# Tokens on two queues, a diagonal in place of scaled tokens, and other numbers of clock products in a two-block forward pass

## The reference

```
# first block
h = concat(meta, x)
xn = rms_norm(h, norm_mix);  proj = xn @ w_in
q, k, v, rw, gate_sb, gate_rw = split(proj)
y_sb = stick_breaking_attention(q, k, v)          # 8 heads
r, kr, vr, w_lo, a_lo, g_lo = split(token_shift(rw))
g = sigmoid(g_lo) @ g_up
y_rw = (group_norm(rwkv7_recurrence(...)) + bonus) * g
h = h + (sigmoid(gate_sb) * (y_sb @ w_sb_out) + sigmoid(gate_rw) * (y_rw @ w_rw_out)) @ w_out
h = h + swiglu(rms_norm(h) @ w_ffn_in) @ w_ffn_out
x = rms_norm(h, norm_final)[16:]
# second block
h = layer_norm(x, ln_in)                           # n = 0
for l in range(2):
    qkv = h @ w_in_2[l];  o = two kinds of attention, normed by head
    h = layer_norm(4 ** 0.25 * h + o @ w_o_2[l], ln1[l])       # n = 1, 3
    w = gelu(h @ u[l]) * gates of the chosen experts
    h = layer_norm(4 ** 0.25 * h + w @ v[l], ln2[l])           # n = 2, 4
return h
```

## Time and profile before

| | |
|---|---|
| device time, median of 3 runs | 2400.44 us (2398.69 to 2403.57) |
| the profiled execution | 2400.53 us |
| its span, from the first to the last instruction | 2398.7 us |
| busy: PE, PE weight loads, DVE, ACT, POOL | 98%, 87%, 70%, 54%, 24% |
| mean granted TensorE clock | 0.996 |
| DMA | 420.99 MB, 176 GB/s in the mean |

### The profile page before, as it was taken

The page is one execution under the profiler, slowest core; times in us unless marked ns, Lnnn a source line. Parts: engine busy times, 40 slices in busy tenths (PEclk is TensorE's granted clock), DMA queues, the critical chain, the costliest instruction groups (busy, mean ns, idle before and its releaser), DMA issues.

```text
span 2398.7 us, 42228 instructions
## 1 busy us (share of the span) xinstructions
PE 2347.3 (98%) x16485; PEld 2095.4 (87%) x16485; DVE 1684.5 (70%) x3068; ACT 1301.3 (54%) x2800; POOL 573.9 (24%) x440
## 2 busy tenths in 40 slices
PE   8999999999999999999999999999999999999998
PEld 7878989997899889999888887789989999888886
DVE  5745354446689778887776556869888888777556
ACT  6543345456564665545555555655665555555554
POOL 3626135555379000000000003378300000000000
PEclk9999999999999999999999999999999999999999
DMA  5311155554245556556776564245555656777554
GB/s 200 116 62 47 54 167 188 187 185 147 75 159 178 190 182 197 193 198 206 244 245 215 193 213 151 82 159 172 182 191 192 194 193 197 237 245 236 194 193 159
DMA packets 148150, 420.99 MB, mean 176 GB/s; under 512 B 15984, under 2 KB 49136, under 8 KB 147568
## 3 DMA queue, kind: packets, MB, share of 16 engines
q1 hardware_dynamic: 144080, 405.34, 51.9%
q0 software_dynamic: 2256, 8.99, 1.0%
q10 hardware_dynamic: 1616, 3.96, 0.4%
HBM read 400.40 MB, written 17.83 MB: 174 GB/s over the span
## 4 chain that ended last, share of the span: by engine, by line
PE 93%; DVE 3%; ACT 2%; POOL 1%; DMA 1%; issue 1%; ACTq 0%; DVEq 0%; SPq 0%
PE pb L465 92%; PE pb L474 1%; POOL lo L2635 1%; ACT arena L1334 1%; ACT hi L1322 0%; DVE arena L2284 0%; ACT arena L1528 0%; DMA cst<-in_consts 0%; DMA raw<-in_w_out 0%; DVE arena L1880 0%; DMA raw<-in_w_ffn_in 0%; DVE arena L1877 0%; DVE arena L2345 0%; ACT HT L1334 0%; ACT L1334 0%
## 5 line engine op out<-in xcount | busy, mean ns | idle before, releaser
L465 PE MATMUL pb<-HT,hi 128*128 128x256 f32 (+2 forms) x5232 | 1093.8, 302 | 3.9 <-POOL lo L2635 1.9
L1322 ACT CAST hi<-raw 128x512 fp32r<-128x512 f32 x1402 | 821.0, 620 | 372.8 <-PE pb L465 255.7
L465 PEld LDWEIGHTS pb<-HT,hi 128*128 128x128 f32 x5232 | 839.0, 191 | 42.6 <-issue 4.3
L465 PE MATMUL pb<-HT,lo 128*128 128x256 f32 (+1 forms) x2968 | 839.3, 283 | 0.0
L2635 POOL TENSOR_TENSOR lo<-raw,hi 128x512 fp32r<-128x512 f32 x384 | 525.3, 1390 | 437.1 <-ACT hi L1322 436.8
L1887 DVE TENSOR_TENSOR lo<-raw,hi 128x1024 fp32r<-128x1024 f32 x464 | 567.4, 1223 | 41.6 <-ACT hi L1322 41.4
L465 PEld LDWEIGHTS pb<-HT,lo 128*128 128x128 f32 x2968 | 566.6, 191 | 0.0
L465 PE MATMUL pb<-hi,WH 128*128 128x512 f32 x1112 | 433.2, 390 | 1.6 <-DVE WL L2569 1.1
L465 PE MATMUL pb<-lo,WH 128*128 128x512 f32 x1112 | 432.9, 389 | 0.0
L465 PE MATMUL pb<-hi,WL 128*128 128x512 f32 x1112 | 432.6, 389 | 0.0
L1334 ACT ACTIVATE arena<-pb 128x256 f32<-128x256 f32 (+2 forms) x216 | 82.4, 382 | 358.6 <-PE pb L465 355.6
(11 more groups left out here) (213 smaller groups left out, 2107.9 us busy)
## 6 DMA issues: line engine op xcount, KB each, us to landing
raw<-in_uT SPq DMA_DIRECT2D x256, 512.0 KB, 3.5
raw<-in_vT SPq DMA_DIRECT2D x256, 512.0 KB, 3.7
raw<-in_w_ffn_in SPq DMA_DIRECT2D x44, 512.0 KB, 3.8
raw<-in_wq SPq DMA_DIRECT2D x32, 512.0 KB, 3.5
wk<-kept SPq DMA_DIRECT2D x128, 128.0 KB, 3.5
raw<-in_w_in SPq DMA_DIRECT2D x24, 512.0 KB, 3.6
raw<-in_w_ffn_out SPq DMA_DIRECT2D x22, 512.0 KB, 4.4
raw<-in_w_gate SPq DMA_DIRECT2D x16, 512.0 KB, 3.2
```

What stands on the lines that cost most here:

```text
L465: return e.matmul(o, l, r, start=start, stop=stop)
L1322: e.copy(u.hi[k], u.half[k]).then_inc(*s.up("hi", ("hi", g)))
```

## The change

- **Start.** Block 0, meta tokens, identity and pack are loaded by ACT in this order; block 1 goes to SP's queue, in front of the weights. POOL waits for block 1 before it issues its four loads. ACT squares only block 0; the mean squares of the meta tokens and of block 1 come from DVE's bn statistics (mean squared plus variance). The tokens are no longer scaled into `xs`: DVE scales the identity into three diagonals `DG`, and PE multiplies the raw tokens (stationary) with the diagonal (moving), which turns and scales in one fp32 product. 18 clock products for 16.
- **Clock products.** Two before each of the four gate sums and two behind `att_c(0)` to `att_c(2)` are new; 44 for 100 at n=0, 20 for 40 at n=1 and n=3, 24 for 50 at n=2.
- **Low parts.** Of the second `w_in` unit of each layer both halves go to POOL.
- **Norms n=1, 3.** Block 0 is closed and scaled before the statistics of piece (1,1); ACT takes two roots; DVE scales (1,0), and ACT only (1,1).
- **Norm n=4.** Gain and bias go into the normalisation: per piece DVE does (x - mean) * gain and then * 1/root + bias, and no other engine works on it.

```diff
-                    low=both if (i, g) < (0, 2) else pool)
+                    low=both if (i, g) < (0, 1) else pool)
...
     w.wait_ge(*s.to("ident"))
-    warm(7, 16)
+    warm(7, 18)
     for c in range(8):
         b = c % 4
         emptied(b)
-        w.wait_ge(*s.to("xs"))
+        w.wait_ge(*s.to("diag"))
         for i, (o, n) in enumerate(BLK):
-            x = tp(PB[b][:, o:o + n], m.xs[0:n, i, c * 128:(c + 1) * 128])
+            x = mm(PB[b][:, o:o + n], m.tok[i][0][:, c * 128:(c + 1) * 128], m.DG[0:n, i * 128:i * 128 + n], True, True)
...
     for f in range(4):
         b, cs = SIDE + f, slice(f * 128, (f + 1) * 128)
         emptied(b)
+        for _ in range(2):
+            mm(PB[b][:, 256:512], m.one[:, 0:128], m.one, True, True)
         w.wait_ge(*s.to("g2"))
...
     for h in range(8):
         att_c(h)
-        if h > 2:
+        if h < 3:
+            warm(2, 2)
+        else:
             att_y(h - 3)
...
-    warm(2, 50)
-    warm(3, 50)
+    warm(2, 22)
+    warm(3, 22)
...
-        warm(2, 20)
-        warm(3, 20)
+        warm(2, 10)
+        warm(3, 10)
...
-            warm(2, 25)
-            warm(3, 25)
+            warm(2, 12)
+            warm(3, 12)
...
     e.dma_start(m.Hv[:, 0, :], rows[:, 0, :]).then_inc(*s.up("x0_in", ("x", 0), by=16))
-    e.dma_start(m.Hv[:, 1, :], rows[:, 1, :]).then_inc(*s.up("x1_in", ("x", 1), by=16))
     e.dma_start(m.meta, m.d["meta_tokens"]).then_inc(*s.up("meta_in", ("meta",), by=16))
-    e.dma_start(m.pk[:, :], m.d["pack"]).then_inc(*s.up("pack_in", by=16))
-    e.dma_start(m.C("ident"), m.d["consts"][:, 0:128]).then_inc(*s.up("pack_in", ("ident",), by=16))
...
+    e.dma_start(m.C("ident"), m.d["consts"][:, 0:128]).then_inc(*s.up("ident_in", ("ident",), by=16))
+    e.dma_start(m.pk[:, :], m.d["pack"]).then_inc(*s.up("pack_in", ("pack",), by=16))
+    w.wait_ge(*s.to("x", 0))
+    fn(m.scr, m.Hv[:, 0, :], ACT.Square, acc=sm[:, 1:2]).then_inc(*s.up("squares", ("sq0",)))
...
+    for i, ready in ((0, ("meta",)), (2, ("x", 1))):
+        x, n = m.tok[i]
+        k, ms = i // 2, sm[0:n, 4 + i:5 + i]
+        w.wait_ge(*s.to(*ready))
+        for j in range(2):
+            e.bn_stats(m.ST6[0:n, k, j, :], x[:, j * 512:(j + 1) * 512]).then_inc(*up("norms"))
+        own()
+        e.bn_aggr(m.MV[0:n, k, :], m.ST6[0:n, k, :, :]).then_inc(*up("norms"))
...
     for i, (x, n) in enumerate(m.tok):
-        ts(m.xs[0:n, i, :], x, sm[0:n, 8 + i:9 + i], None, M).then_inc(*up("norms", *([("xs",)] if i == 2 else [])))
+        x = ts(m.DG[0:n, i * 128:i * 128 + n], C("ident")[0:n, 0:n], sm[0:n, 8 + i:9 + i], None, M)
...
+    def attention_norm(n, pieces, ready, src):
...
+        statistics(HALVES[:3], pieces, ready, src)
+        block_root(0)
+        block_inverse(0)
+        scaled(n, 0, 0, src(0, 0))
+        statistics([(1, 1)], pieces, ready, src)
+        block_root(1)
+        scaled(n, 0, 1, src(0, 1))
+        block_inverse(1)
+        shift(n)
+        scaled(n, 1, 0, src(1, 0))
...
+    def output_norm(pieces, ready, src):
+        statistics([(0, 0), (0, 1), (1, 0), (1, 1)], pieces, ready, src)
+        means(0, 1)
+        root_of(4)
+        w.wait_ge(*s.to("bc", 4))
+        for i, (t, k) in enumerate([(0, 0), (0, 1), (1, 0), (1, 1)]):
+            cs, bs = slice(k * 512, (k + 1) * 512), slice(1024 + k * 512, 1536 + k * 512)
+            stt(m.FP[:, t, cs], src(t, k), m.MV[:, t, 0:1], m.BC2[:, cs], S, M).then_inc(*up("last"))
+            if i == 0:
+                inverse(4)
+            own()
+            x = stt(m.Hv[:, t, cs], m.FP[:, t, cs], sm[:, 102 + t:103 + t], m.BC2[:, bs], M, A)
...
     d = m.d
+    w.wait_ge(*s.to("x", 1))
     e.dma_start(m.lora, d["lora"]).then_inc(*s.up("lora_in", by=16))
...
+    e.dma_start(m.Hv[:, 1, :], rows[:, 1, :]).then_inc(*s.up("x1_in", ("x", 1), by=16))
     for i, u in enumerate(m.units):
```

More of the change, by code:

```diff
@@ L1302, in tensor @@
         emptied_by({(0, k): OUTV[0, k] for k in range(2)}, ("pre", l, 1))
-        for k in range(2):
-            free[OUTV[1, k]] = [("hn", 2 * l + 2, 1, k)]
         if l == 0:
-            warm(2, 25)
-            warm(3, 25)
+            for k in range(2):
+                free[OUTV[1, k]] = [("hn", 2, 1, k)]
+        if l == 0:
+            warm(2, 12)
+            warm(3, 12)
 def scalar(e, s, m):
@@ L1781, in scalar @@
         root_table()
-        norm_root(2 * l + 1, [m.XN[:, 1, 0:512], PB[OB[1, 1]][:, :]])
+        n = 2 * l + 1
+        for t in range(2):
+            w.wait_ge(*s.to("var_eps", n, t))
+            fn(sm[:, 102 + t:103 + t], sm[:, 100 + t:101 + t], ACT.Sqrt).then_inc(*s.up("roots", ("ln_root", n, t)))
+        w.wait_ge(*s.to("shift", n))
+        x = fn(m.Hv[:, 1, 512:1024], PB[OB[1, 1]][:, :], ACT.Identity, scale=sm[:, 103:104], bias=m.SHIFT)
+        x.then_inc(*s.up("norms_act", ("hn", n, 1, 1)))
         turned_biased(("exp", l), f"g1{l}", f"b1{l}", ("in", l), TURNS_EXP)
@@ L1852, in scalar @@
         root_table()
-        norm_root(2 * l + 2, [PB[OUTV[1, k]][:, :] for k in range(2)])
-    for t, k in HALVES:
+        if l == 0:
+            norm_root(2, [PB[OUTV[1, k]][:, :] for k in range(2)])
+    w.wait_ge(*s.to("var_eps", 4))
+    fn(sm[:, 102:104], sm[:, 100:102], ACT.Sqrt).then_inc(*s.up("roots", ("ln_root", 4)))
+    for t, k in ((0, 0), (0, 1), (1, 0), (1, 1)):
         cs = slice(k * 512, (k + 1) * 512)
@@ L1904, in vector @@
     own()
-    for i in (1, 2, 0):
-        n = m.tok[i][1]
-        w.wait_ge(*s.to("sq0", i))
-        ts(sm[0:n, 4 + i:5 + i], sm[0:n, i:i + 1], 1.0 / 1024, 1e-6, M, A).then_inc(*up("norms", *([] if i else [("ms0",)])))
+    for i, ready in ((0, ("meta",)), (2, ("x", 1))):
[7 more added lines that the diff above has]
+        own()
+        stt(ms, m.MV[0:n, k, 0:1], m.MV[0:n, k, 0:1], m.MV[0:n, k, 1:2], M, A).then_inc(*up("norms"))
+        own()
+        ts(ms, ms, 1.0, 1e-6, M, A).then_inc(*up("norms"))
+    w.wait_ge(*s.to("sq0"))
+    ts(sm[:, 5:6], sm[:, 1:2], 1.0 / 1024, 1e-6, M, A).then_inc(*up("norms", ("ms0",)))
     w.wait_ge(*s.to("root0"))
@@ L1911, in vector @@
     own()
+    w.wait_ge(*s.to("ident"))
     for i, (x, n) in enumerate(m.tok):
-        ts(m.xs[0:n, i, :], x, sm[0:n, 8 + i:9 + i], None, M).then_inc(*up("norms", *([("xs",)] if i == 2 else [])))
+        x = ts(m.DG[0:n, i * 128:i * 128 + n], C("ident")[0:n, 0:n], sm[0:n, 8 + i:9 + i], None, M)
+        x.then_inc(*up("norms", *([("diag",)] if i == 2 else [])))
+    w.wait_ge(*s.to("pack"))
     for c in range(8):
@@ L2196, in vector, with statistics @@
             take("fout", j - 1)
-    def layer_norm(n, order, pieces, ready, src, extra=None):
+    def statistics(order, pieces, ready, src):
         def stats(t, k):
@@ L2207, in layer_norm, with means, root_of @@
                 stats(*order[i - 1])
-        stats(*order[3])
+        stats(*order[-1])
+    def means(*ts_):
         own()
-        for t in range(2):
+        for t in ts_:
             e.bn_aggr(m.MV[:, t, :], m.ST6[:, t, :, :]).then_inc(*up("stats"))
         own()
+    def root_of(n, extra=None):
         if extra is None:
@@ L2220, in layer_norm, with shift, scaled, input_norm @@
         own()
+    def shift(n):
         stt(m.SHIFT, m.MV[:, 1, 0:1], -1.0, sm[:, 103:104], M, M).then_inc(*up("stats", ("shift", n)))
-        for k in range(2):
-            cs = slice(k * 512, (k + 1) * 512)
-            x = ts(m.Hv[:, 0, cs], src(0, k), m.MV[:, 0, 0:1], sm[:, 102:103], S, M)
-            x.then_inc(*up("norms", ("hn", n, 0, k)))
+    def scaled(n, t, k, src):
+        cs = slice(k * 512, (k + 1) * 512)
+        x = ts(m.Hv[:, t, cs], src, m.MV[:, t, 0:1], sm[:, 102 + t:103 + t], S, M)
+        x.then_inc(*up("norms", ("hn", n, t, k)))
+    def input_norm(n, order, pieces, ready, src, extra=None):
+        statistics(order, pieces, ready, src)
+        means(0, 1)
+        root_of(n, extra)
+        inverse(n)
+        shift(n)
+        for k in range(2):
+            scaled(n, 0, k, src(0, k))
+    def attention_norm(n, pieces, ready, src):
+        def block_root(t):
+            means(t)
+            ts(sm[:, 100 + t:101 + t], m.MV[:, t, 1:2], 1e-5, None, A).then_inc(*up("stats", ("var_eps", n, t)))
+        def block_inverse(t):
+            w.wait_ge(*s.to("ln_root", n, t))
+            e.reciprocal(sm[:, 102 + t:103 + t], sm[:, 102 + t:103 + t]).then_inc(*up("stats"))
+            own()
+        statistics(HALVES[:3], pieces, ready, src)
[6 more added lines that the diff above has]
+        block_inverse(1)
+        shift(n)
+        scaled(n, 1, 0, src(1, 0))
+    def output_norm(pieces, ready, src):
+        statistics([(0, 0), (0, 1), (1, 0), (1, 1)], pieces, ready, src)
+        means(0, 1)
+        root_of(4)
[5 more added lines that the diff above has]
+                inverse(4)
+            own()
+            x = stt(m.Hv[:, t, cs], m.FP[:, t, cs], sm[:, 102 + t:103 + t], m.BC2[:, bs], M, A)
+            x.then_inc(*up("last", ("y_out", t, k)))
```

37 lines of the change are left out of this document (12 added, 25 removed).

## The result

The changed kernel took 2392.60 us (median of 7 runs, 2390.78 to 2401.89) against 2400.44 us (7 runs, 2398.69 to 2404.00): ratio 0.9971, 95% interval 0.9962 to 0.9981. That is 7.8 us faster, inside the predicted range and 3.3 us above the forecast. In a later session the same kernel took 2395.53 us against 2401.87 us, ratio 0.9961 (0.9943 to 0.9979); its single runs spread over 11 us, more than any term of the sum, and much of what follows is about that. In that session 2395.53 us lies 0.9 us above the predicted range, while the kernel before was 1.4 us slower than in the first.

The account below looks back on a forecast made before the run. The chain of waits runs 93% through TensorE, so time is won only where PE stands or does needless work. -0.5 + 1.5 - 5.8 - 2.2 - 2.7 - 1.5 = -11.2 us from 2400.5 gave 2389.3 us; range 2385.0 to 2394.6.

Parts of the forecast that it names:

- main term: The largest term of the sum: at the norm n=0, PE turns from 543.8 instead of 549.58 us, -5.8 us.
- Start: Kernel start: identity at 6.9 us, tokens from 11.0 us, main products near 18.8 us; -0.5 us (bounds -2.8 and +1.5).
- Added clock products: 8 in the gate sums, 6 in the first attention, at 0.111 us each: +1.5 us (bounds +0.5 and +1.6).
- n=0: First normalisation: 44 clock products instead of 100, PE turns from 543.8 instead of 549.58 us: -5.8 us.
- the rival of the eaten gain: Gain of the norms is eaten by the next wait, POOL's low part at 559.68 us: 2400.0 us, chance 0.09.
- n=1 and n=3: Norms with 20 clock products and a new order, itself 0.2 us slower: -1.1 us, twice (bounds 0 and -2.1).
- the rival of the fallen clock: Clock falls in two norms, n=1 and n=3, for 5 us each, costing 2.5 us apiece: 2394.3 us, chance 0.14.
- n=2: DVE's low part goes to POOL, 24 clock products; PE turns at 1469.3 instead of 1472.00 us: -2.7 us.
- End: Final DVE chain: eight fused steps of 0.72 us and a reciprocal end at 2394.7 us: -1.5 us (bounds -0.5 and -1.9).
- the slower case: Clock stays down at every norm, 10.1 us at the low level at each of four: 2409.5 us, chance 0.06.
- fourfold: Rival at the start: the diagonal costs four transposes, +10.0 us against the sum's term: 2399.3 us, chance 0.03.
- The lucky rival: Level products keep their clock by luck or moved phase: up to 5 us more, 2384.3 us, chance 0.08.

Follow-up runs that it names:

- run 13: No run label: words from "A rare run 13 us above the rest", single slow runs of the kernel before and of both kernels without the 14 added clock products.

## Why the prediction was right, and where not

The direction, the range and the main term held; the working was off in several places.

That the median lies inside the range is in part luck. Two of the seven runs rose late; in the later session five of twelve did, and the median of 2395.53 us lies outside it. The sum knew nothing of the late rise. It fits the runs that rose early, with medians of 2392.3 and 2392.8 us in the two sessions, still 3 to 3.5 us above 2389.3. Nor do the bounds of the single terms give the 2385 to 2393 us that the text names: taken all at once they give 2383.5 to 2396.9.

- **Start**, forecast -0.5, measured +0.18. Two errors. The landings: the identity came at 7.83 us instead of 6.9 and meta at 6.97 instead of 6.1, so the step that scaled the time behind block 0 by the bytes ahead was 0.9 us short, and all behind it moved by the same 1.0 us (diagonals at 11.98 for 11.0). Its 197.5 KB also count the pack, which in the change stands behind the identity; with the 128 KB left the step would have said 6.5 us and been 1.3 us short. The upper bound of 9 us allowed for it. And the 0.87 us wait for DVE went, as said; the price of the diagonals was right (7.52 us for 7.6). What the step did not have at all is that it ran on a clock that had only just risen: late, the same 24 products take 13.2 us. The text took the clock at the start as given because the trace of before showed it up at 14.3 us. It was a rival to look for, and the largest one.
- **Added clock products**, forecast +1.5, measured +0.90: one between other work costs about 0.07 us, not the 0.111 us of a long row of them. Up to n=0 another 0.33 us was lost in the rms norm, a wait that the sum had at nothing. What the sum lacks as well is the other side of these 14: without them some runs take 13 us more.
- **n=0**, forecast -5.8, measured -5.62. The wait for POOL moved along, so the rival of the eaten gain is refuted by the row at 555.48 us. The padding alone gives 5.0 of it.
- **n=1 and n=3**, forecast -1.1 each. This is the step that failed. By itself -0.46 and -0.48, since "the new order is 0.2 us slower" should have read 1.0 us: the order puts the first scale beside POOL's low part, where it takes 1.46 us, and all behind it waits. POOL's row stood in the trace of before beside other work of DVE, and I costed every scale at its length alone. Then the clock: the rival of the fallen clock came in at half its price, at both norms, 1.3 and 1.4 us. With it the two norms together cost 1.8 us instead of giving 2.2. The rival had weighed the standing in front of PE's transposes rightly and its price was too high; whether its chance, 0.14, was too low the runs don't tell, for a second profile of the same kernel showed neither fall.
- **n=2**, forecast -2.7, measured -2.58. The experiment with the padding alone bears its cause out: without the low part's move it would have been 0.4 to 0.7 us.
- **End**, forecast -1.5, measured -1.60, with the last step 6.0 us behind the small one (forecast 6.2).
- **The other rivals**: no clock fell at n=0 or n=2 in the changed kernel, so the slower case had no place; a 128x128 step of the diagonal products takes 5.7/32 = 0.18 us, two of them 0.36 beside a transpose's 0.22, and nothing is fourfold.
- **The lucky rival** (the level products keep their clock) came true in other traces: of fourteen, eight, the kernel before and the changed one among them, have 10.2 us at 1.2 GHz there, four have 6.8 and two 3.4 us. The kernel with 45 and 24 early clock products is one of the two, and takes 185.9 us from 157.97 to 343.83 us, where the changed kernel of its session takes 188.0 us for the same work.

## What to carry to other kernels

When padding that keeps the clock up is cut, cut it to the moment at which the next real work is ready and not below: here every clock product past that moment cost 0.11 us, while PE's standing for 1.5 to 2.1 us before transposes was followed by 3.41 us at 1.2 GHz at six of thirteen places, a loss of 1.2 to 1.4 us at the three where it was read off. Padding between other work can be worth its price though the median shows only the price: look at the longest runs too. Look at the start of a kernel as at a norm: padding from a cleared tile before the first transfer lands put the first main product at 20.03 and 20.45 us where the second profile of the changed kernel has 19.75, and once it left PE no pause the spread of the runs went from 9.2 to 2.8 us; a median over runs that spread so far says little about edits of 1 us. Before moving a DVE step forward, see whether POOL is busy there.

## What was not expected of the hardware

- **The clock's rise differs from run to run.** With 18 clock products from 7.8 to 8.3 us on it rose at 11.5, 11.8 and 12.3 us in three traces, and at 24.5, 27.1 and 27.3 us in three others. In the late ones PE did small fp32 products or transposes, with hardly a break, from 12 or 14 us on and stayed at 1.2 GHz through all of them; the rise came only 1.5 to 3.8 us into the main products. Once up, the clock stayed up through the same products. So in these traces steps that held the clock did not raise it. The Trainium skill, "TensorE: Matmul & The Clock Gate", Part 4, says that a transpose doesn't count as PE-busy the same way. The run with transposes agrees for the rise (not up from 13.95 to 20.71 us), rows 11 speak against it for the holding, and the fp32 products with the diagonal behaved as the transposes did, which the rule doesn't say.
- **A DVE scale beside POOL.** 128x512 in fp32 from SBUF to SBUF took 0.54 us alone and 1.45 to 1.47 us beside POOL's subtraction of 1.26 us, at twelve of the fourteen norms n=1 and n=3 in the seven traces with the new order. At the other two it started 0.4 us ahead of POOL's subtraction and took 0.69 and 0.72 us, while the subtraction took 1.45 and 1.46 us; there it was 5.34 and 5.21 us to the first product behind the norm instead of 5.91 to 5.99. The stretched scale is two thirds of what the order costs. Statistics beside the same POOL work kept their 0.67 to 0.69 us. The Trainium skill, "SBUF — State Buffer", section "SBUF: two separate sides", says that DVE's two-port modes and POOL lock a shared port pair for a whole instruction. The trace agrees: POOL's last two subtractions take 2.51 us from 649.93 us, so the last runs from about 651.18 to 652.44 us, and the scale, which starts at 651.26 us, ends at 652.72 us, just behind it. Whether the scale ran in a two-port mode no row shows.
- **A rare run 13 us above the rest** in the kernel before (2412 to 2416 us) and in both kernels without the added clock products (2401 to 2403 us). Its mean granted clock is 0.989 to 0.992 for 0.994 to 0.998, so its time goes to the low clock. Where it falls and what sets it off stays open, as do the 0.51 us of the table between n=2 and n=3.
